# First MoE's combine inside the projection phase's tile loop, with a diagonal for 1/rms

## The chip, the cores and the metric

One NeuronCore of a Trainium2 chip runs the whole program once. The metric is device time in microseconds (us) of that execution, lower is better; a kernel is stated by the median of its runs. Engines are named as the profile names them: PE is TensorE, with its weight loads apart as PEld; DVE is VectorE, ACT is ScalarE, POOL is GpSimd, SP is SyncE, which here only starts DMA transfers.

## The reference

A two-layer decoder over T = 1040 tokens (16 meta tokens and 1024 of the input) of width 1024. Layer 0 is a state-space mixer and a mixture of experts (MoE). After it one K/V projection and layer 1's queries are taken from the residual stream `h`; layer 1 is a windowed attention and a second MoE. What matters here is how layer 0's MoE ends and what reads it:

```python
# hier_moe: every token goes to two of 32 experts
contrib = yb[dest] * sgate[:, None].astype(yb.dtype)
out = jnp.zeros_like(t).at[stok].add(contrib)

# reference
h = h + hier_moe(rmsnorm(h, norm_ffn[layer]), ...)          # layer 0
...
shared = shared_kv(rmsnorm(h, norm_kv), w_kv, b_kv)         # K and V, 256 columns each
q = (rmsnorm(h, norm_mix[1]) @ w_q + b_q)                   # 1024 columns

def rmsnorm(x, g):
    y = xf * lax.rsqrt(jnp.mean(xf * xf, axis=-1, keepdims=True) + RMS_EPS)
    return (y * g)
```

All three projections start from `h / rms(h)`; only the gains `norm_kv` and `norm_mix[1]` differ, and the kernel multiplies them into the weights.

## The kernel before

The program is a row of phases (`phase_mixer`, `phase_moe` for layer 0, `phase_project`, `phase_attend`, `phase_moe` for layer 1). Each phase is a block with one hand-written instruction stream for each engine; the streams meet only in semaphores, and at the end of a phase all engines meet, the phase's semaphores are cleared and the next block begins. So the order on each engine is that of the code. Tokens lie in 9 tiles: tiles 0 to 7 of 128 tokens, tile 8 (`XT`) of the 16 meta tokens. Float32 products are made of three passes over halves: a value is split into `hi` (ACT copies it to a rounded type) and `lo` (DVE subtracts), and PE adds hi·hi, lo·hi and hi·lo.

**End of `phase_moe`, layer 0.** Expert tiles are processed in a loop; each ends with a `down` product, an ACT copy to `y` (`store_y`, L1208) and a scatter by POOL to `y_dram` (L1129), of which one may be open at a time (`y_free`). When the last scatter has landed, SP loads for each token tile the pair of its expert outputs, 1 MB, into the place of the weight staging `raw` (L1040, six places, `NB`), and DVE adds them to `h` with the token's two gates (L1461, two instructions a tile). That is the combine. Then the phase ends.

**`phase_project`.** SP loads gains, three 512 KB column blocks of weights and biases. A loop over the 9 tiles follows: ACT squares the tile and sums (L1739), POOL makes `1/rms` in two small instructions (L1717, L1720), DVE multiplies `xn = h * rstd` (L1780), PE transposes it in eight pieces (L1827), ACT copies the result to `x_hi` (L1754), DVE subtracts to `x_lo` (L1771). POOL multiplies the gain into the first three weight blocks between the tiles (L1711). After the loop come the products, 12 column blocks of weights in order: K0, K1, then V (two blocks together, nine jobs of 128 or 16 tokens), then Q0 to Q7. The staging `raw` has three slots, `w_hi` and `w_lo` two each. A weight block passes through load (SP, after `w_lo_done` of the block three back), gain (POOL), `w_hi` (ACT, after PE has finished the block two back) and `w_lo` (DVE), and PE waits for that before its products (L1848). K and Q products have the weight as stationary operand and 512 tokens as moving one, V products have a token tile as stationary and 256 columns of weights as moving operand, 24 matmuls a job. DVE takes each result out of PSUM with its bias (L1805 for K, L1808 for V, L1810 for Q). In `phase_attend` PE runs for a while `spare_products(6)` (L2169), six plain float32 matmuls (ahead of the loop twelve, in one go) of 128 columns that nobody reads; the trace holds two rows for each of them.

Of the kernel before, what the change touches and what calls it, by code (L numbers as in the profile page):

```python
# [46 lines left out]

def tile_rows(i):

    return P if i < XT else N_META  # L50


def semaphore_source(nc, ctx, prefix):

    sems = []
# [10 lines left out]
    return sem  # L66

# [768 lines left out]
def phase_moe(nc, t, layer, out=None):  # L836
# [27 lines left out]
    with ExitStack() as ctx:  # L864
# [7 lines left out]

        ident = sb("ident", [P, P])
# [13 lines left out]
        gates = sb("gates", [P, 2, NT])  # L887
# [33 lines left out]
        raw = sb("raw", [P, 6, KC * F])  # L921
        hi, lo = (sb(x, [P, 3, KC * F], F32R) for x in ("hi", "lo"))
# [32 lines left out]
        yc_in = [sem(f"yc_in{b}") for b in range(NB)]  # L955
# [23 lines left out]
        def _(sp):  # L979
# [177 lines left out]
        def _(act):  # L1157
# [84 lines left out]
            store_y(n_q - 2, n_q * 6)  # L1242
            store_y(n_q - 1, n_q * 6 + 2)
# [8 lines left out]
        def _(dve):  # L1252
# [195 lines left out]
            hidden_lo_part(n_q - 1)  # L1448

# [7 lines left out]
            for i in range(NT):  # L1457
# [157 lines left out]
def phase_project(nc, t):  # L1615
# [7 lines left out]
    NP = 2 * KV // P + DC  # L1623
    K_P, V_P = KV // P, 2 * KV // P
    h, q_t, k_t, v_sb = t["h"], t["q_t"], t["k_t"], t["v_sb"]
    w_kv = t["w_kv"].rearrange("(p c) f -> p c f", c=DC)
    w_q = t["w_q"][0].rearrange("(p c) f -> p c f", c=DC)
    with ExitStack() as ctx:
        def sb(name, shape, dt=F32):
            return ctx.enter_context(nc.sbuf_tensor("prj_" + name, shape, dt))  # L1630

        sem = semaphore_source(nc, ctx, "prj_")
# [3 lines left out]
        sq = sb("sq", [P, D])  # L1636
        xn = sb("xn", [P, 2, D])
# [3 lines left out]
        g_kv, g_q = (sb(x, [P, DC]) for x in ("g_kv", "g_q"))  # L1641
        raw = sb("raw", [P, 3, DC, P])
        w_hi, w_lo = (sb(f"w_{x}", [P, 2, DC, P], F32R) for x in ("hi", "lo"))
        bk = sb("bk", [P, K_P])
# [5 lines left out]
        w_in = [sem(f"w_in{b}") for b in range(3)]  # L1650
        gains_in, bias_in, k_copied = (sem(x) for x in ("gains_in", "bias_in", "k_copied"))
        const_set, ident_step, squares_done, ss_scaled, rstd_done, xn_done, xt_mm, xt_hi, xt_lo = (
            sem(x) for x in ("const_set", "ident_step", "squares_done", "ss_scaled", "rstd_done", "xn_done",
# [19 lines left out]
        def _(sp):  # L1673
            def load(n):
                src = w_kv[:, :, n * P:(n + 1) * P] if n < V_P else w_q[:, :, (n - V_P) * P:(n - V_P + 1) * P]
                sp.dma_start(raw[:, n % 3], src).then_inc(w_in[n % 3], 16)

            for dst, src in ((g_kv, t["norm_kv"]), (g_q, t["norm_mix"][1])):
                sp.dma_start(dst[:, :], src.rearrange("(p c) -> p c", c=DC)).then_inc(gains_in, 16)
            for n in range(3):  # L1680
                load(n)
            sp.dma_start(bk[:, :], t["b_kv"][0:KV].rearrange("(c p) -> p c", p=P),
                         allow_slow_non_contiguous=True).then_inc(bias_in, 16)
            sp.dma_start(bq[:, :], t["b_q"][0].rearrange("(c p) -> p c", p=P),
                         allow_slow_non_contiguous=True).then_inc(bias_in, 16)
            sp.dma_start(bv[:, :], t["b_kv"][KV:].partition_broadcast(P)).then_inc(bias_in, 16)
            sp.wait_ge(squares_done, NT)
            sp.dma_start(sq[:, :], t["b_o"][0].partition_broadcast(P)).then_inc(bo_in, 16)
            for n in range(3, NP):
                sp.wait_ge(w_lo_done, n - 2)  # L1690
                load(n)
                if n == V_P:

                    sp.wait_ge(acc_free, jobs_before(K_P))
# [7 lines left out]
        def _(pool):  # L1702
# [3 lines left out]
            pool.wait_ge(gains_in, 32)  # L1706

            def gain(n):
                g = g_kv if n < V_P else g_q
                pool.wait_ge(w_in[n % 3], 16 * (n // 3 + 1))  # L1710
                nc.gpsimd.tensor_tensor(raw[:, n % 3], raw[:, n % 3],  # L1711
                                        g[:, :].unsqueeze(2).to_broadcast([P, DC, P]), ALU.mult).then_inc(gained, 1)

            for i in range(NT):
                n = tile_rows(i)
                pool.wait_ge(squares_done, i + 1)
                nc.gpsimd.tensor_scalar(ss[0:n, i:i + 1], ss[0:n, i:i + 1], 1.0 / D, EPS,  # L1717
                                        ALU.mult, ALU.add).then_inc(ss_scaled, 1)
                pool.wait_ge(ss_scaled, i + 1)
                nc.gpsimd.tensor_tensor(rstd[0:n, i:i + 1], ss[0:n, i:i + 1], mhalf[0:n, :],  # L1720
                                        ALU.pow).then_inc(rstd_done, 1)
                if i < 3:
                    gain(i)
            pool.wait_ge(bo_in, 16)
            pool.wait_ge(xn_done, NT)
            for n in range(3, NP):
                gain(n)
                if n >= V_P:
                    i = n - V_P
                    nc.gpsimd.tensor_tensor(h[:, i, :], h[:, i, :], sq[:, :], ALU.add).then_inc(bo_added, 1)  # L1730
# [3 lines left out]
        def _(act):  # L1734
            def squares(i):
                n = tile_rows(i)
                if i:
                    act.wait_ge(squares_done, i)
# [17 lines left out]
            for n in range(NP):  # L1756
                split_w(n)
# [468 lines left out]
```

## Time and profile before

| | us |
|---|---|
| median of the three runs (2241.44 to 2243.8) | 2242.67 |
| time of the execution that was profiled | 2243.16 |
| span of that execution in the trace | 2241.4 |
| PE busy in it | 1985.4 (89%) |
| DVE busy | 1586.7 (71%) |
| ACT busy | 1244.6 (56%) |
| POOL busy | 369.5 (16%) |
| last matmul of layer 0's MoE to first transpose of the projection: idle time of PE | 40.0 |
| first transpose to first product of the projection | 30.8 |
| first product to the end of the last | 152.3 |
| end of DVE's half of the last expert's fourth weight block (`lo_done` at `n_q * 6 - 2`), at | 1044.8 |

Times of instructions are microseconds from the start of the span. The profile is one execution. A timeline row gives start, length, engine, line, operation, tensors, shapes and the count of merged instructions; in square brackets stands how long the engine had been idle and who ended that. A matmul's length in a row holds its way through the array, so in a stream of matmuls the distance between starts tells more than the lengths. PEclk is the clock granted to PE, 1.00 for 2.4 GHz and 0.50 for 1.2 GHz.

### The profile page before, as it was taken

The page shows a single profiled execution, that of the slowest core. Times are in us where ns is not written, and L with a number is a line of the kernel's source. Part 1 is how long each engine was busy: PE and PEld are TensorE (multiplying, and loading weights), DVE is VectorE, ACT ScalarE, POOL GpSimd, SP SyncE. Part 2 cuts the span into 40 slices and gives each one's busy share as a digit, 9 for nine tenths or more (in the row PEclk, how much of TensorE's full clock was granted, in tenths as well). Part 3 has the DMA queues.
Part 4 walks back from the last instruction along what each step waited for, and adds up shares of the span by engine and source line. Part 5 has one row for each costly group of instructions (what it writes and reads, how often), then busy time and mean ns, then how long its engine had stood idle before and what let it go on. Part 6 is the DMA issues. An engine that isn't in the chain of part 4 may idle for free. (4 is left out here: it accounts for less than half of the span.)

```text
span 2241.4 us, 31742 instructions
## 1 busy us (share of the span) xinstructions
PE 1985.4 (89%) x10658; PEld 1572.3 (70%) x10658; DVE 1586.7 (71%) x1770; ACT 1244.6 (56%) x1521; POOL 369.5 (16%) x684
## 2 busy tenths in 40 slices
PE   4859999659999999999189999998599999999991
PEld 3558777548888888887178766666388888888880
DVE  8995221558888888887642276663688888888885
ACT  6524110437777777776120065554277777777772
POOL 2000000302211112221224000002022212112214
PEclk9979999879999999999579999999699999999995
DMA  3265100639999999996521020005299999999985
GB/s 98 36 60 176 63 1 1 248 113 365 381 375 371 367 373 374 377 376 253 189 67 38 10 86 1 1 1 198 103 343 360 360 375 385 378 384 387 383 315 235
DMA packets 136045, 504.69 MB, mean 225 GB/s; under 512 B 38466, under 2 KB 68498, under 8 KB 84754
## 3 DMA queue, kind: packets, MB, share of 16 engines
q1 hardware_dynamic: 116258, 468.85, 57.4%
q0 software_dynamic: 18432, 33.86, 4.0%
q10 hardware_dynamic: 1280, 0.98, 0.3%
q8 instruction: 47, 0.77, 0.1%
q14 instruction: 28, 0.23, 0.0%
HBM read 488.47 MB, written 47.32 MB: 239 GB/s over the span
## 5 line engine op out<-in xcount | busy, mean ns | idle before, releaser
L1406 DVE TENSOR_TENSOR moe_lo<-moe_raw,moe_hi 128x2048 fp32r<-128x2048 f32 x378 | 861.0, 2292 | 118.4 <-ACT moe_hi L1191 114.1
L1191 ACT CAST moe_hi<-moe_raw 128x2048 fp32r<-128x2048 f32 x374 | 714.2, 1915 | 153.5 <-PE moe_ps_g L1546 74.9
L1544 PE MATMUL moe_ps_g<-moe_hi,moe_x_hi 128*128 128x512 f32 x512 | 211.6, 413 | 7.2 <-DVE moe_x_lo L1411 4.7
L1544 PE MATMUL moe_ps_y<-moe_hi,moe_h_hi 128*128 128x512 f32 x512 | 209.0, 408 | 3.7 <-DVE moe_h_lo L1422 3.7
L1545 PE MATMUL moe_ps_g<-moe_hi,moe_x_lo 128*128 128x512 f32 x512 | 205.8, 402 | 0.0
L1546 PE MATMUL moe_ps_g<-moe_lo,moe_x_hi 128*128 128x512 f32 x512 | 205.3, 401 | 0.0
L1545 PE MATMUL moe_ps_y<-moe_hi,moe_h_lo 128*128 128x512 f32 x512 | 204.2, 399 | 0.0
L1546 PE MATMUL moe_ps_y<-moe_lo,moe_h_hi 128*128 128x512 f32 x512 | 203.9, 398 | 0.0
L1546 PE MATMUL moe_ps_u<-moe_lo,moe_x_hi 128*128 128x512 f32 x512 | 203.0, 396 | 0.0
L1544 PE MATMUL moe_ps_u<-moe_hi,moe_x_hi 128*128 128x512 f32 x512 | 202.8, 396 | 0.0
L1545 PE MATMUL moe_ps_u<-moe_hi,moe_x_lo 128*128 128x512 f32 x512 | 202.8, 396 | 0.0
L1198 ACT CAST moe_x_hi<-moe_ps_xt 128x1024 fp32r<-128x1024 f32 x64 | 65.1, 1017 | 157.2 <-PE moe_ps_xt L1531 157.2
L1544 PEld LDWEIGHTS moe_ps_g<-moe_hi,moe_x_hi 128*128 128x128 f32 x512 | 99.2, 194 | 29.9 <-DVE moe_x_lo L1411 5.5
L1411 DVE TENSOR_TENSOR moe_x_lo<-moe_ps_xt,moe_x_hi 128x1024 fp32r<-128x1024 f32 x64 | 78.4, 1225 | 52.3 <-ACT moe_x_hi L1198 52.3
L1544 PEld LDWEIGHTS moe_ps_y<-moe_hi,moe_h_hi 128*128 128x128 f32 x512 | 97.5, 191 | 25.2 <-DVE moe_lo L1406 4.0
L1546 PEld LDWEIGHTS moe_ps_g<-moe_lo,moe_x_hi 128*128 128x128 f32 x512 | 98.2, 192 | 24.0
L1546 PEld LDWEIGHTS moe_ps_y<-moe_lo,moe_h_hi 128*128 128x128 f32 x512 | 97.0, 189 | 23.6
L1545 PEld LDWEIGHTS moe_ps_u<-moe_hi,moe_x_lo 128*128 128x128 f32 x512 | 96.7, 189 | 23.6
L1545 PEld LDWEIGHTS moe_ps_g<-moe_hi,moe_x_lo 128*128 128x128 f32 x512 | 98.6, 192 | 20.9
L1544 PEld LDWEIGHTS moe_ps_u<-moe_hi,moe_x_hi 128*128 128x128 f32 x512 | 96.4, 188 | 23.5
L1546 PEld LDWEIGHTS moe_ps_u<-moe_lo,moe_x_hi 128*128 128x128 f32 x512 | 96.4, 188 | 23.2
L1545 PEld LDWEIGHTS moe_ps_y<-moe_hi,moe_h_lo 128*128 128x128 f32 x512 | 97.2, 190 | 20.7
(406 smaller groups left out, 3699.1 us busy)
## 6 DMA issues: line engine op xcount, KB each, us to landing
moe_raw<-moe_w_gate SPq DMA_DIRECT2D x128, 1024.0 KB, 7.3
moe_raw<-moe_w_up SPq DMA_DIRECT2D x128, 1024.0 KB, 8.0
moe_raw<-moe_w_down SPq DMA_DIRECT2D x128, 1024.0 KB, 7.3
moe_raw<-y_dram SPq DMA_DIRECT2D x16, 1024.0 KB, 11.6
mix_r<-ssm_w_glu SPq DMA_DIRECT2D x16, 512.0 KB, 5.2
xn_dram<-moe_work SPq DMA_DIRECT2D x16, 512.0 KB, 7.4
mix_r<-x SPq DMA_DIRECT2D x8, 512.0 KB, 5.4
mix_r<-h_dram SPq DMA_DIRECT2D x16, 256.0 KB, 11.6
```

Source lines behind the costliest of these rows:

```text
L1191: A.copy(hi[:, slot(number, k), :], raw[:, k, :]).then_inc(hi_done, 1)
L1198: A.copy(x_hi[:, :, :].rearrange("p c m -> p (c m)"), ps_xt[:, :]).then_inc(xt_hi, 1)
L1406: V.tensor_tensor(lo[:, slot, :], raw[:, k, :], hi[:, slot, :].bitcast(F32), ALU.subtract).then_inc(lo_done, 1)
L1411: V.tensor_tensor(x_lo[:, :, :].rearrange("p c m -> p (c m)"), ps_xt[:, :], x_hi[:, :, :].bitcast(F32).rearrange("p c m -> p (c m)"), ALU. ...
L1544: T.matmul(out, x_h, w_h, start=first, stop=False)
L1545: T.matmul(out, x_l, w_h, start=False, stop=False)
L1546: return T.matmul(out, x_h, w_l, start=False, stop=final)
```

## The change

It does four things.

1. The combine leaves `phase_moe` of layer 0. SP still issues the first four pair loads there, into `yc`, a ring of four places (`N_YC`) over memory that held `hi` and `lo`; the other five are issued in `phase_project`, each after the tile four back is combined. The semaphores `yc_in` and the tensors `gates`, `yc` outlive the phase. Tiles now come in the order 8, 0, 1 to 7 (`TILE_ORDER`).
2. In the tile loop DVE combines a tile, and the product `xn = h * rstd` is gone. DVE instead writes `scale`, the identity times `rstd` (128x128), and PE multiplies `h` by it, which transposes and scales at once: eight plain float32 matmuls in the place of eight transposes.
3. The V products of a tile (24 matmuls) follow in the same loop, one tile behind; DVE takes them out of PSUM in the loop too. V comes before K.
4. The four weight blocks of K and V are loaded, multiplied by their gain (now by DVE) and split at the end of `phase_moe`, after the last expert's halves. Weights have a ring of four slots (`W_KV`), with `w_lo` written in place over `w_raw`. A Q block's load waits until PE has finished the block four back.

The biases and the query gain are loaded by ACT's queue; `b_o` and the squares use the memory of `gain`.

```diff
@@ phase_moe
+                sp.dma_start(g_kv[:, :], t["norm_kv"].rearrange("(p c) -> p c", c=DC)).then_inc(wkv_in, 16)
+                sp.wait_ge(lo_done, n_q * 6 + (-2))
+                for n in range(W_KV):
+                    sp.dma_start(t["w_raw"][:, n], kv_columns(t, n)).then_inc(wkv_in, 16)
             sp.wait_ge(y_free, n_q + 1)
-            for i in range(NT):
+            if not last_layer:
+                for j in range(N_YC):
+                    load_pair(sp, t, j)
+            for i in range(NT if last_layer else 0):
...
             store_y(n_q - 2, n_q * 6)
+            if not last_layer:
+                for n in range(W_KV):
+                    act.wait_ge(gained, n + 1)
+                    A.copy(t["w_hi"][:, n], t["w_raw"][:, n]).then_inc(wkv_hi, 1)
             store_y(n_q - 1, n_q * 6 + 2)
...
             hidden_lo_part(n_q - 1)
+            if not last_layer:
+                dve.wait_ge(wkv_in, 16 * (W_KV + 1))
+                for n in range(W_KV):
+                    V.tensor_tensor(t["w_raw"][:, n], t["w_raw"][:, n], g_kv[:, :].unsqueeze(2).to_broadcast([P, DC, P]),
+                                    ALU.mult).then_inc(gained, 1)
+                for n in range(W_KV):
+                    dve.wait_ge(wkv_hi, n + 1)
+                    V.tensor_tensor(t["w_lo"][:, n], t["w_raw"][:, n], t["w_hi"][:, n].bitcast(F32),
+                                    ALU.subtract).then_inc(wkv_lo, 1)
@@ phase_project, SP
+            for j in range(N_YC, NT):
+                sp.wait_ge(h_new, 2 * (j - N_YC + 1))
+                load_pair(sp, t, j)
             sp.wait_ge(squares_done, NT)
             sp.dma_start(sq[:, :], t["b_o"][0].partition_broadcast(P)).then_inc(bo_in, 16)
-            for n in range(3, NP):
-                sp.wait_ge(w_lo_done, n - 2)
-                load(n)
+            for n in range(Q0, NC):
+                sp.wait_ge(acc_done, jobs_to(n - W_KV))
+                sp.dma_start(w_raw[:, n % W_KV], w_q[:, :, (n - Q0) * P:(n - Q0 + 1) * P]).then_inc(w_in[n % W_KV], 16)
@@ phase_project, ACT
+            for j in range(NT):
+                squares(j)
+                if j >= 1:
+                    hi_part(j - 1)
+            hi_part(NT - 1)
@@ phase_project, DVE
-                V.tensor_scalar(xn[0:n, i % 2, :], h[0:n, i, :], rstd[0:n, i:i + 1], None,
-                                ALU.mult).then_inc(xn_done, 1)
+            def set_scale(j):
+                i = TILE_ORDER[j]
+                n = tile_rows(i)
+                dve.wait_ge(rstd_done, j + 1)
+                if j >= 2:
+                    dve.wait_ge(xt_mm, j - 1)
+                V.tensor_scalar(scale[0:n, j % 2, 0:n], ident[0:n, 0:n], rstd[0:n, i:i + 1], None,
+                                ALU.mult).then_inc(scale_set, 1)
...
+            for j in range(NT + 3):
+                if j < NT:
+                    combine(j)
+                if 1 <= j <= NT:
+                    set_scale(j - 1)
+                if 2 <= j <= NT + 1:
+                    lo_part(j - 2)
+                if j == 3:
+                    dve.wait_ge(bias_in, 48)
+                if j >= 3:
+                    values(j - 3)
@@ phase_project, PE
-                for c in range(DC):
-                    last = T.transpose(ps_x[:, i % 2, c * P:c * P + n],
-                                       xn[0:n, i % 2, :].rearrange("p (m c) -> p c m", c=DC)[:, c, :],
-                                       ident[0:n, 0:n])
+                for c in range(DC):
+                    last = T.matmul(ps_x[:, j % 2, c * P:c * P + n],
+                                    h[0:n, i, :].rearrange("p (m c) -> p c m", c=DC)[:, c, :],
+                                    scale[0:n, j % 2, 0:n], start=True, stop=True)
...
+            for j in range(NT):
+                turn(j)
+                if j >= 1:
+                    value_product(j - 1)
+            value_product(NT - 1)
```

DVE's instructions from the last expert's half into the projection phase. Before (`moe_h_lo` is that half, L1461 the combine, L1780 the scaled tile):

```order
L1422 TENSOR_TENSOR moe_h_lo<-moe_ps_ht,moe_h_hi 128x512
L1461 SCALAR_TENSOR_TENSOR h<-moe_raw,moe_gates,h 128x1024 x16
L1461 SCALAR_TENSOR_TENSOR h<-moe_raw,moe_gates,h 16x1024 x2
L864 UNCONDITIONAL_BRANCH
L1759 UNCONDITIONAL_BRANCH
L1780 TENSOR_SCALAR prj_xn<-h,prj_rstd 128x1024 x2
L1771 TENSOR_TENSOR prj_x_lo<-prj_ps_x,prj_x_hi 128x8x128
```

And in the changed kernel, up to the first full round of the loop:

```order
L1460 TENSOR_TENSOR moe_h_lo<-moe_ps_ht,moe_h_hi 128x512
L1490 TENSOR_TENSOR w_raw<-w_raw,moe_g_kv 128x1024 x4
L1494 TENSOR_TENSOR w_lo<-w_raw,w_hi 128x1024 x4
L886 UNCONDITIONAL_BRANCH
L1797 UNCONDITIONAL_BRANCH
L1806 SCALAR_TENSOR_TENSOR h<-yc,gates,h 16x1024 x2
L1806 SCALAR_TENSOR_TENSOR h<-yc,gates,h 128x1024 x2
L1816 TENSOR_SCALAR prj_scale<-prj_ident,prj_rstd 16x16
L1806 SCALAR_TENSOR_TENSOR h<-yc,gates,h 128x1024 x2
L1816 TENSOR_SCALAR prj_scale<-prj_ident,prj_rstd 128x128
L1823 TENSOR_TENSOR prj_x_lo<-prj_ps_x,prj_x_hi 128x8x16
L1806 SCALAR_TENSOR_TENSOR h<-yc,gates,h 128x1024 x2
```

The combine crossed the phase's end and now alternates with the scale and the halves; the eight weight instructions stand in its old place.

SP's queue at the same place. Before:

```order
L1030 DMA moe_raw<-moe_w_down 128x2048
L1036 REGISTER_ALU
L1040 DMA moe_raw<-y_dram 128x2048 x8
L1040 DMA moe_raw<-y_dram 16x2048
L864 UNCONDITIONAL_BRANCH
L1672 UNCONDITIONAL_BRANCH
L1679 DMA prj_g_kv<-norm_kv 128x8
L1679 DMA prj_g_q<-norm_mix 128x8
L1676 DMA prj_raw<-w_kv 128x8x128 x3
```

And in the changed kernel:

```order
L1055 DMA moe_raw<-moe_w_down 128x2048
L1062 DMA moe_g_kv<-norm_kv 128x8
L1063 REGISTER_ALU
L1065 DMA w_raw<-w_kv 128x8x128 x4
L1067 REGISTER_ALU
L86 DMA yc<-y_dram 16x2048
L86 DMA yc<-y_dram 128x2048 x3
L886 UNCONDITIONAL_BRANCH
L1719 UNCONDITIONAL_BRANCH
L86 DMA yc<-y_dram 128x2048 x5
L1725 DMA gain<-b_o 128x1024
L1728 DMA w_raw<-w_q 128x8x128 x4
```

The weight loads stand ahead of the pair loads, and five of the nine pair loads stand behind the phase's end.

## Rows read from the trace of the kernel before

**Rows 1.** Stretches: us, busy PE, PEld, DVE, ACT, POOL, PEclk, DMA share, GB/s.
```profile
1070.00:1103.00 33.00, 0.00 (x0) 0.00 (x0) 23.10 (x18) 2.30 (x4) 0.95 (x5) 0.50 0.64 260
1103.00:1135.00 32.00, 16.79 (x72) 13.51 (x72) 20.88 (x20) 17.59 (x25) 12.21 (x20) 0.50 0.25 68
```

**Rows 2.** Timelines of SP, DVE and POOL over the phase's end; start us, length us.
```profile
1069.75 3.06 SPq L1040 DMA_DIRECT2D moe_raw<-y_dram  x6
...
1074.44 18.45 DVE L1461 SCALAR_TENSOR_TENSOR h<-moe_raw,moe_gates,h 128x1024 f32<-128x1024 f32 x14 [17.76 <-DMA moe_raw<-y_dram]
1093.74 5.22 DVE L1461 SCALAR_TENSOR_TENSOR h<-moe_raw,moe_gates,h 128x1024 f32<-128x1024 f32 x4 [0.84 <-DMA moe_raw<-y_dram]
...
1100.30 0.10 POOL L1703 MEMSET prj_mhalf<- 128x1 f32 x1 [30.57 <-POOLq L59]
```

**Rows 3.** Timeline of PE: first products of K0, of V, of Q0.
```profile
1135.10 0.77 PE L1848 MATMUL prj_acc<-prj_x_hi,prj_w_hi 128*128 128x512 f32 x1 [2.65 <-DVE prj_w_lo L1765]
...
1167.27 0.55 PE L1848 MATMUL prj_acc<-prj_w_hi,prj_x_hi 128*128 128x256 f32 x1 [2.50 <-DVE prj_w_lo L1765]
...
1198.15 0.50 PE L1848 MATMUL prj_acc<-prj_x_hi,prj_w_hi 128*128 128x512 f32 x1 [2.45 <-DVE prj_w_lo L1765]
```

**Rows 4.** Timeline: ACT's square, DVE's half, PE's eight transposes; POOL's `b_o` after it.
```profile
1122.70 1.06 ACT L1739 ACTIVATE prj_sq<-h 128x1024 f32<-128x1024 f32 x1
...
1125.56 1.23 DVE L1771 TENSOR_TENSOR prj_x_lo<-prj_ps_x,prj_x_hi 128x1024 fp32r<-128x1024 f32 x1
...
1125.60 1.97 PE L1827 MATMUL prj_ps_x<-prj_ident,prj_xn 128*128 128x128 f32 x8 [1.12 <-DVE prj_xn L1780]
...
1144.18 2.41 POOL L1730 TENSOR_TENSOR h<-h,prj_sq 128x1024 f32<-128x1024 f32 x1
```

**Rows 5.** Timeline of PE: twelve plain float32 matmuls in 24 rows, and eight transposes.
```profile
1289.75 2.94 PE L2169 MATMUL att_ps_y<-att_ident 128*128 128x128 f32 x24
...
1612.79 1.05 PE L1531 MATMUL moe_ps_xt<-moe_ident,moe_xg 128*128 128x128 f32 x8
```

**Rows 6.** Timeline of DVE: K's and V's results taken out of PSUM.
```profile
1162.22 1.78 DVE L1805 TENSOR_SCALAR k_t<-prj_acc,prj_bk 64x384 f32<-64x384 f32 x4 [3.78 <-PE prj_acc L1848]
1164.80 1.08 DVE L1805 TENSOR_SCALAR k_t<-prj_acc,prj_bk 64x16 f32<-64x16 f32 x6 [0.80 <-PE prj_acc L1848]
...
1175.97 0.43 DVE L1808 TENSOR_TENSOR v_sb<-prj_acc,prj_bv 128x256 f32<-128x256 f32 x1 [2.78 <-PE prj_acc L1848]
1178.81 0.42 DVE L1808 TENSOR_TENSOR v_sb<-prj_acc,prj_bv 128x256 f32<-128x256 f32 x1 [2.42 <-PE prj_acc L1848]
```

**Rows 7.** Stretches, PE alone (busy, PEclk, DMA share, GB/s): V's start, all of Q.
```profile
1167.20:1173.40 6.20, 6.13 (x29) 0.50 1.00 239
...
1198.10:1287.40 89.30, 89.24 (x384) 1.00 0.10 30
```

**Rows 8.** Timelines of DVE and POOL in the second MoE's combine, at its end.
```profile
2213.78 2.60 DVE L1461 SCALAR_TENSOR_TENSOR h<-moe_raw,moe_gates,h 128x1024 f32<-128x1024 f32 x2
...
2215.20 1.59 POOL L1154 TENSOR_TENSOR moe_rstd<-moe_ss,moe_mhalf 128x1 f32<-128x1 f32 x1
...
2234.38 0.55 POOL L1154 TENSOR_TENSOR moe_rstd<-moe_ss,moe_mhalf 128x1 f32<-128x1 f32 x1
```

**Rows 9.** End of the first MoE: DVE, ACT, POOL, and the K/V weight loads' landing.
```profile
1055.99 0.68 DVE L1422 TENSOR_TENSOR moe_h_lo<-moe_ps_ht,moe_h_hi 128x512 fp32r<-128x512 f32 x1
...
1064.36 1.01 ACT L1211 COPY moe_y<-moe_ps_y 128x1024 f32<-128x1024 f32 x1 [7.74 <-PE moe_ps_y L1546]
...
1065.53 0.18 POOL L1113 COPY moe_si<-moe_idx_out 128x1 int32 x1 [4.48 <-ACT moe_y L1211]
...
prj_raw<-w_kv SPq DMA_DIRECT2D x4, 512.0 KB, 5.7
```

**Rows 10.** Stretches of the second MoE's routing, all engines, columns as in Rows 1.
```profile
1555.00:1565.00 10.00, 7.88 (x64) 6.85 (x63) 6.44 (x8) 8.10 (x9) 2.60 (x4) 1.00 1.02 427
1565.00:1575.00 10.00, 7.02 (x43) 5.70 (x43) 7.57 (x15) 3.04 (x3) 0.00 (x0) 0.83 1.01 402
```

More of the change, by code:

```diff
@@ L1455, in final_scale @@
                                        ALU.mult).then_inc(fin_done, 1)
-            for i in range(NT):
+            for i in range(NT if last_layer else 0):
                 n = rows(i)
@@ L1640, in phase_project @@
         x_hi, x_lo = (sb(f"x_{x}", [P, DC, TOK], F32R) for x in ("hi", "lo"))
[L1641 to L1644, printed above, removed]
+        g_q = sb("g_q", [P, DC])
+        bk = sb("bk", [P, K0])
         bq = sb("bq", [P, DC])
@@ new lines, in hi_part @@
+            def hi_part(j):
+                i = TILE_ORDER[j]
+                n = tile_rows(i)
+                act.wait_ge(xt_mm, j + 1)
+                A.copy(x_hi[:, :, i * P:i * P + n],
+                       ps_x[:, j % 2, :].rearrange("p (c m) -> p c m", c=DC)[:, :, 0:n]).then_inc(xt_hi, 1)
+            for j in range(NT):
[3 more added lines that the diff above has]
+            hi_part(NT - 1)
+            for n in range(Q0, NC):
+                act.wait_ge(gained, n - Q0 + 1)
+                A.copy(w_hi[:, n % W_KV], w_raw[:, n % W_KV]).then_inc(w_hi_done, 1)
@@ L1787, in _ @@
-            k = 0
-            for n in range(NP):
-                ahead = n + 1 < NP and n != V_P - 1
-                if ahead:
+            dve.wait_ge(ident_step, 2)
+            for j in range(NT + 3):
[9 more added lines that the diff above has]
+                    values(j - 3)
@@ L1791, in _ @@
+            k = NT
+            for n in range(K0, NC):
+                if Q0 <= n + 1 < NC:
                     split_w(n + 1)
@@ new lines, in value_product @@
+            def value_product(j):
+                pe.wait_ge(xt_lo, j + 1)
+                i = TILE_ORDER[j]
+                product(j, 0, i * P, tile_rows(i))
+            for j in range(NT):
[3 more added lines that the diff above has]
+            value_product(NT - 1)
+            k = NT
+            for n in range(K0, NC):
+                if n >= Q0:
+                    pe.wait_ge(w_lo_done, n - Q0 + 1)
+                for at, m in jobs(n):
+                    product(k, n, at, m)
@@ L2206, in program @@
         phase_mixer(nc, t)
+        t["gates"] = ctx.enter_context(nc.sbuf_tensor("gates", [P, 2, XT + 1], F32))
+        t["yc"] = nc.alloc_sbuf_tensor_at("yc", [P, N_YC, 2, D], F32, offset=-(-nc.sbuf_base // 32) * 32)
+        for name, at, dt in (("w_raw", RAW_AT + 2 * 8192, F32), ("w_lo", RAW_AT + 2 * 8192, F32R),
+                             ("w_hi", RAW_AT + 4 * 8192, F32R)):
+            t[name] = nc.alloc_sbuf_tensor_at(name, [P, W_KV, DC, P], dt, offset=at)
+        t["yc_in"] = [nc.alloc_semaphore(name=f"yc_in{b}") for b in range(N_YC)]
         phase_moe(nc, t, 0)
```

232 lines of the change are left out of this document (112 added, 120 removed).

## The prediction, made before the result was known

> **What bounds the kernel now.** Read the stretches first. Between 1070 and 1103 us PE does nothing, and between 1103 and 1135 it is busy 16.8 of 32 us with transposes at a clock of 0.50 [rows 1]. So the edge between the first MoE and the products costs some 65 us, in which PE has little to do, and every microsecond of it is on the path, since nothing of the later phases can start.
>
> The timelines say what ends last in it. The scatter is through at 1069.7, the first pair of expert outputs lands 4.7 us after its issue, DVE combines from 1074.44 to 1098.96, and 1.34 us later the next phase begins [rows 2]. Then the tile loop runs, and PE starts on products at 1135.10. Two more waits lie in the weight pipeline, 2.50 us before V and 2.45 before Q [rows 3]; after the first of them the clock is 0.50 again for 6.2 us [rows 7]. From 1198.1 to 1287.4 the Q products run without a gap at 1.00 [rows 7]; there nothing can be gained.
>
> **What the change takes away.** I don't add up savings but build the new time line from 1069.7 to the end of the Q products, 1287.4 before, and take the difference.
>
> *End of the MoE.* The V weights now have to be split before this edge. The K/V loads took 5.7 us at the median [rows 9]; four are issued from 1044.8 on (the table's last line), 11 us before DVE's last half at 1055.99 [rows 9], and should have landed. DVE's four gains and four halves are the size of L1771's, 1.23 us [rows 4], 9.8 us together, and run from 1056.7 to 1066.5, in time in which DVE was idle. What hides them is the last `down` product and the scatter; ACT's four copies (1.01 us each, as its copy of `y` of the same size, so through at about 1062.7) stand ahead of that last copy of `y` at 1064.36 [rows 9], with 1.6 us to spare. One thing is not hidden. In the second MoE's combine a POOL instruction of 0.55 us takes 1.59 while DVE works on two tensors in SBUF [rows 8]; it ends only when DVE's instruction has ended. POOL's step before the last scatter, 1065.53 [rows 9], now meets DVE's last half, which ends at 1066.5. I charge 0.9 us (bounds 0 and 3, if POOL's instructions of the scatter before meet DVE as well and the y buffer comes free late).
>
> *Start of the loop.* First load issued at 1070.65; four issues at 0.51 us (six in 3.06 [rows 2]) to 1072.7; 1.34 for the phase's end, 1074.0. The first data can be there at 1070.65 + 4.7 = 1075.3, which is later. A tile's combine is 2 x 1.32 = 2.64 us (14 in 18.45 [rows 2]). Tiles 8 and 0 are combined by 1080.6. The 1/rms of the first one is held up by DVE as above, so that the scale comes 0.8 later, 1081.4 (the scale itself is not in the trace; `xn` with eight times the columns bounds it at 0.75 us, I take 0.2). Third combine 1084.0, scale 0.6 later: PE can turn the first full tile at 1084.6.
>
> *The loop.* DVE has per tile 2.64 + 0.2 + 1.23 + 0.42 = 4.5 us [rows 2, 4, 6]. PE has the turn and the V job. The V job is 2.84 us, from one result to the next [rows 6]. The turn is eight plain float32 matmuls of 128 columns with 128-column weights. The nearest row is of just that form: twelve of them take 2.94 us, so eight take 1.96; eight transposes take 1.05 [rows 5], the lower bound. Sum 4.8 us, so PE is the bound, by a little. It should run almost without gaps from 1084.6, because `turn` of the next tile fills the time in which ACT and DVE make the halves of this one, and its own need is met in time: counted from the end of turn j-2, DVE gets the V result at 2.84 and has the scale of tile j ready 0.42 + 2.64 + 0.2 later, at 6.1, while PE wants it at 2.84 + 1.96 + 2.84 = 7.6. So 8 turns 15.7 us, 9 V jobs 25.6 us (the one for 16 tokens streams the same columns), waits of 0.1 a tile 0.8 us. It starts at half clock. Before V the clock rose after 6.2 us of work [rows 7], before K after 4; that loses 3.1 or 2.0 us, I take 2.6. The last V job ends at 1084.6 + 15.7 + 25.6 + 0.8 + 2.6 = 1129.3.
>
> *K and Q.* A job of 24 matmuls with 512 columns takes 89.3 / 16 = 5.57 us [rows 7], one with 16 columns 2.58 [rows 6]. K is 4 x 5.57 + 2 x 2.58 = 27.5, Q 89.1. With four slots Q0's load starts at the end of V and has the 27.5 us of K to pass through load (5.7), gain and `b_o` on POOL (2.4 each at most [rows 4]), copy and half (2.2); later blocks have more than 11 us of slack. So no waits: 1129.3 + 27.5 + 89.1 = 1245.9.
>
> 1287.4 - 1245.9 = 41.5 us less. The profiled execution would go from 2243.2 to 2201.7, and since the median of the runs lies 0.5 below it, I predict 2201 us.
>
> **POOL and DVE.** [Rows 8] speak against the change: in the old loop DVE's `xn` reads one SBUF tensor, in the new one the combine reads two, and it is on while POOL makes 1/rms. The Trainium skill states it too (GPSIMD Engine Reference, Specifications): GpSimd's way to SBUF is shared with VectorE, with contention when a DVE instruction has two SBUF inputs. The trace agrees, 1.59 us for 0.55. In steady state it costs nothing by my order: after combine j DVE has 1.9 us of scale, half and V result, while the square takes 1.06 [rows 4] and its sum a little more, and POOL 0.8, and the scale is needed only after combine j+1.
>
> **The price of a plain float32 matmul.** The transposes that go are cheap and what replaces them is not: 1.96 against 1.05 us [rows 5]. The Trainium skill (TensorE: Matmul & The Clock Gate, Terms) says that the transpose mode is four times as fast for FP32. By that the turn would cost 4.2 us instead of 1.96, 17.9 more over eight tiles, 2219 us. The row of the same form says no; I keep it as a rival.
>
> **The rivals.**
>
> A, the forecast: the loop runs at PE's pace of 4.8 us. 2201, own range 2195 to 2208. 70%.
>
> B, the loop goes at the pace of a chain instead: scale held up by POOL (up to 1.0), the half waiting for ACT, which stands behind a square. Then a tile takes 5.4 to 6.5 us; seven intervals more at 0.6 to 1.7 are 4 to 12 us, 2205 to 2213. For it: the two engines are so close (4.5 and 4.8) that any delay shows. Against: the 1.5 us of slack just counted. 13%.
>
> C, PE's clock stays at 0.50 through the loop. V jobs 24 x 6.13 / 29 = 5.1 us [rows 7], turns 1.97 [rows 4] x 1.96 / 1.05 = 3.7. Then 8 x 3.7 + 9 x 5.1 = 75.5 after 1084.6, end at 1160.1 + 2.5 to warm up + 116.6 = 1279.2, 8 less than before: 2234. For it: with PE 70% busy the clock was 0.83 [rows 10], so it falls where gaps come. Against: at half clock PE is behind and has no gaps at all, which is how it rose before K and V, and at 79% busy it was granted 1.00 [rows 10]. 5%.
>
> D, slower than before: half clock, and PE waits each tile for copy and half of the same tile (1.01 + 1.23). Then a tile takes 3.7 + 5.1 + 2.2 = 11.0 us. It decides at 10.0 us a tile: 1084.6 + 7 x 10.0 + 13.9 + 119.1 = 1287.6, the old end. At 11.0 the time is 2250. Against it stands that `turn` of the next tile is ahead of the V job in PE's order. 3%.
>
> E, better than forecast: turns near 1.05 us. Then DVE's 4.5 is the pace, the end of V is 1084.6 + 7 x 4.5 + 1.1 + 5.7 = 1122.9, 6.4 earlier, 2195; with no loss at the scatter 2194. 7%.
>
> F, the turn at 4.2 us as above, 2219. 2%.
>
> That the change doesn't do what it says has a small form only: if the K/V blocks landed after 1060, ACT's last copy of `y` would wait for `w_hi` and all would move by that. It is in A's range.
>
> **How the numbers follow.** Range 2193 to 2213: it holds nearly all of A, B and E and leaves out C, D, F and the tails, somewhat under 20%. Faster by more than 0.2% (4.5 us, about what a measurement can tell from no change): A, B, C, E and F, 96 to 97%; slower D, 3%; in between about 1%, between C and D.
>
> **What would show it.** Right: turns of about 2 us and V jobs every 4.8 to 4.9 us on PE between 1085 and 1130, clock 1.00 after the first tiles; last V result near 1129; no wait for `w_lo` after it; Q's end near 1246. DVE should wait for ACT's copy, not PE for the scale. Wrong: POOL's two instructions at 1.3 to 1.6 us in steady state with PE waiting behind the scale (B); PEclk of 0.5 between 1090 and 1125 (C, D); turns of 1 or of 4 us (E, F); ACT's last copy of `y` later than 1064.4.

## The result, and the profile after

| | before | after |
|---|---|---|
| median of the runs shown, us | 2243.24 (4 runs, 2241.44 to 2245.32) | 2214.11 (4 runs, 2212.98 to 2215.36) |
| span of the profiled execution | 2241.4 | 2212.9 |
| start of the projection phase on POOL | 1100.30 | 1076.39 |
| last V result taken out of PSUM, start | 1195.74 | 1143.44 |
| last Q result taken out of PSUM, start | 1287.43 | 1260.73 |

The ratio is 0.987, with a 95% interval of 0.9856 to 0.9884: 29.1 us less, where 41.5 were forecast. The forecast time was 2201, with a range to 2213; the median lies 1.1 above that. Three of the stations in the table carry the reading: V's end was forecast at 1129.3 and came at 1143.4; from there to Q's end took 117.3 us, where 116.6 were forecast. So nearly the whole miss lies ahead of V's end (14.1 us there, 0.7 behind it).

PE's timeline of the changed kernel, the rows of the turn (those of V between them are left out):

```profile
1083.16 8.00 PE L1886 MATMUL prj_ps_x<-prj_scale,h 16*128 16x16 f32 x32 [20.13 <-DVE prj_scale L1816]
...
1093.81 3.98 PE L1886 MATMUL prj_ps_x<-prj_scale,h 128*128 128x128 f32 x16
...
1100.45 3.98 PE L1886 MATMUL prj_ps_x<-prj_scale,h 128*128 128x128 f32 x16
...
1107.11 3.98 PE L1886 MATMUL prj_ps_x<-prj_scale,h 128*128 128x128 f32 x16
```

One turn is 16 rows, two for each of eight matmuls, and it stands every 6.66 us. V's share of that is 2.82, so a turn is 3.84, not 1.96. The row that I had taken the price from [rows 5] is one of *the same shape and type*. The difference shows in the weight loads, in the groups of the two lines (shortest, median and longest length in ns, first and last start); the second group holds the spare products of [rows 5] in the changed kernel:

```profile
L1886 PEld LDWEIGHTS prj_ps_x<-prj_scale,h x144: 307/336/338, 1083.2 to 1137.2; 128*128 128x128 f32 x128, 16*128 16x128 f32 x16
```

```profile
L2242 PEld LDWEIGHTS att_ps_y<-att_ident x120: 186/192/192, 1263.1 to 1290.4; 128*128 128x128 f32 x120
```

DVE's timeline of one round answers to [rows 4, 6]:

```profile
1107.65 2.60 DVE L1806 SCALAR_TENSOR_TENSOR h<-yc,gates,h 128x1024 f32<-128x1024 f32 x2
1110.29 0.29 DVE L1816 TENSOR_SCALAR prj_scale<-prj_ident,prj_rstd 128x128 f32<-128x128 f32 x1
1112.17 1.23 DVE L1823 TENSOR_TENSOR prj_x_lo<-prj_ps_x,prj_x_hi 128x1024 fp32r<-128x1024 f32 x1 [1.60 <-ACT prj_x_hi L1785]
1113.97 0.42 DVE L1831 TENSOR_TENSOR v_sb<-prj_acc,prj_bv 128x256 f32<-128x256 f32 x1 [0.57 <-PE prj_acc L1904]
```

It works 4.5 us a round and waits for 2.2, first for ACT's copy of the turn, then for V: both times PE is behind it. The stretches say the same (busy us of PE, PEld, DVE, ACT, POOL, then PEclk, DMA share, GB/s): PE has no gap.

```profile
1084.00:1100.00 16.00, 16.00 (x91) 15.42 (x91) 10.46 (x13) 5.44 (x9) 4.77 (x7) 0.80 0.65 235
1100.00:1110.00 10.00, 10.00 (x59) 10.00 (x57) 7.16 (x9) 2.06 (x3) 1.45 (x4) 1.00 0.11 48
1110.00:1120.00 10.00, 10.00 (x66) 10.00 (x66) 6.12 (x8) 4.12 (x6) 0.81 (x3) 1.00 0.00 0
```

The phase's edge, which answers to [rows 2, 9], is the second place. POOL's timeline:

```profile
1057.02 1.09 POOL L1147 COPY moe_si<-moe_idx_out 128x1 int32 x1 [9.04 <-ACT moe_y L1245]
1058.18 1.06 POOL L1150 TENSOR_TENSOR moe_unit<-moe_mhalf 128x1 f32<-128x1 f32 x1
1059.39 1.81 POOL L1163 DMA_INDIRECT y_dram<-moe_y,moe_si  x1
...
1066.47 1.00 POOL L1163 DMA_INDIRECT y_dram<-moe_y,moe_si  x1
1069.80 0.18 POOL L1167 TENSOR_TENSOR moe_unit<-moe_mhalf 128x1 f32<-128x1 f32 x1 [2.33 <-DMA y_dram<-moe_y,moe_si]
1076.39 0.10 POOL L1740 MEMSET prj_mhalf<- 128x1 f32 x1 [6.40 <-POOLq L65]
```

And the instruction that fills that idle time, in the group of the phase's block (it stands once at the end of each MoE):

```profile
L886 POOLq DRAIN  x2: 5560/5740/5919, 1069.8 to 2205.8; - x2
```

SP had issued its four pair loads by 1071.8; then every engine waits for POOL's DRAIN until 1075.4. The kernel before has it too, from 1069.5 to 1075.1: there it lay under the wait for the first pair (until 1074.44) and the first instruction of the combine [rows 2].

### The profile page after: what moved, and what is told of

Read it like the earlier page. It is cut to its first block and busy times, and to the rows that moved or that the text cites. A ratio compares the mean times of both kernels' runs of the same rounds, so it can differ in the third digit from the quotient of the medians.

```text
span 2212.9 us, 31883 instructions
## 1 busy us (share of the span) xinstructions
PE 1993.8 (90%) x10730; PEld 1586.2 (72%) x10730; DVE 1582.4 (72%) x1774; ACT 1243.6 (56%) x1521; POOL 368.4 (17%) x680
```

## The experiments

Unless said otherwise each differs from the changed kernel by its edit alone, and its output is the reference's. "Round" is the distance between two combines in DVE's timeline. The profiled executions differ ahead of this place too: the projection phase starts on POOL at 1073.18 in `e4_v_after` and at 1076.39 in the changed kernel, with the same code up to there. So stations of two kernels are compared from the phase's start on, not from the span's.

### The turn's price: where the columns lie

The turn reads `h` as its stationary operand with every eighth column (`"p (m c) -> p c m"`); the spare products of [rows 5] read neighbouring ones. The first experiment gives the channels another order, so that the eight pieces are neighbouring columns, and loads `w_kv`, `w_q` and the two gains in that order. Theory S is the stride.

```diff
-    return t["w_kv"].rearrange("(p c) f -> p c f", c=DC)[:, :, at:at + P]
+    return t["w_kv"].rearrange("(c p) f -> p c f", c=DC)[:, :, at:at + P]
...
-                                    h[0:n, i, :].rearrange("p (m c) -> p c m", c=DC)[:, c, :],
+                                    h[0:n, i, c * P:(c + 1) * P],
```

> The changed kernel with one thing different: the projection's channels are taken as (c p) in the place of (p c), for weights, gains and the turn, so that the turn's stationary operand is 128 neighbouring columns of h and not every eighth one. What is computed is the same. Theory S (the stride of the stationary operand is what makes the turn take 3.84 us instead of 1.96): the turn's weight loads take 0.19 us instead of 0.34, the turn 1.9 us, a tile 4.8 us instead of 6.66, and the median falls by 8 x 1.86 = 15 us, from 2214 to 2199. Rival P (a plain float32 matmul on h costs 0.48 us however the operand lies, the cheap row was a special case): no change, 2214.

2199.45 us, ratio 0.9798 (0.9782 to 0.9815). PE's timeline:

```profile
1095.86 1.95 PE L1888 MATMUL prj_ps_x<-prj_scale,h 128*128 128x128 f32 x16
...
1100.47 1.95 PE L1888 MATMUL prj_ps_x<-prj_scale,h 128*128 128x128 f32 x16
...
1105.07 1.95 PE L1888 MATMUL prj_ps_x<-prj_scale,h 128*128 128x128 f32 x16
```

The same 16 rows take 1.95 us where they took 3.98, both by the row's length, and the forecast from [rows 5] was 1.96. A round is 4.61, so that by distance, without V's 2.82, a turn is 1.79. Now DVE waits 0.21 us a round in all, so the two engines stand as close together as the prediction had them.

The second measures the form by itself. Behind the twelve spare products ahead of the attention's loop it adds eight groups of twelve more, on `q_t`, that nobody reads: neighbouring columns of `q_t`, then every 2nd, 4th and 8th, transposes of neighbouring ones and of every 8th, and `q_t` as moving operand with neighbouring columns and with every 8th. The first group is:

```diff
+            for _ in range(12):
+                T.matmul(ps_y[:, 0:P], qf[:, 0:P], ident[:], start=True, stop=True)
...
```

> The changed kernel with eight groups of twelve unused matmuls of 128 columns put behind the twelve spare ones ahead of the attention, one form to a line: plain float32 with 128 columns of q as stationary operand, neighbouring, then every second, every fourth, every eighth; two groups of transposes, neighbouring and every eighth; two plain ones with the identity as stationary and q as moving operand, neighbouring and every eighth. The output is not touched. Theory S (stride of the stationary operand of a plain float32 matmul): group 1 at 0.24 us a matmul, group 4 at 0.48, transposes 0.12 in both, moving stride no effect or a smaller one; groups 2 and 3 tell whether the price grows with the stride or comes at once. Rival P (data other than the identity): group 1 already at 0.48.

One run, 2241.63 us beside 2243.91 before it. PE's timeline:

```profile
1262.70 2.94 PE L2242 MATMUL att_ps_y<-att_ident 128*128 128x128 f32 x24
1265.48 2.84 PE L2251 MATMUL att_ps_y<-att_ident,q_t 128*128 128x128 f32 x24
1268.16 2.99 PE L2253 MATMUL att_ps_y<-att_ident,q_t 128*128 128x128 f32 x24
1270.99 5.76 PE L2255 MATMUL att_ps_y<-att_ident,q_t 128*128 128x128 f32 x24
1276.59 5.87 PE L2257 MATMUL att_ps_y<-att_ident,q_t 128*128 128x128 f32 x24
1282.30 1.47 PE L2259 MATMUL att_ps_y<-att_ident,q_t 128*128 128x128 f32 x12
1283.61 1.50 PE L2261 MATMUL att_ps_y<-att_ident,q_t 128*128 128x128 f32 x12
1284.94 2.84 PE L2263 MATMUL att_ps_y<-q_t,att_ident 128*128 128x128 f32 x24
1287.62 5.76 PE L2265 MATMUL att_ps_y<-q_t,att_ident 128*128 128x128 f32 x24
```

Read the distances between starts; the clock was 1.00 throughout. Neighbouring columns (L2242, L2251) and every second (L2253) cost 2.7 to 2.8 us for twelve matmuls; every fourth and eighth (L2255, L2257) 5.6 to 5.7. As moving operand (L2263, L2265) it is the same, 2.7 and 5.7, where I had expected no effect or a smaller one. Transposes (L2259, L2261) cost 1.3 either way. A step of 4 or 8 columns doubles a plain float32 matmul, a step of 2 doesn't (3 wasn't tried), and a step of 8 leaves a transpose alone. Why the step costs this wasn't tried. That settles theory S; its rival fell with the first of the two experiments.

### The second part undone: DVE makes `xn`, PE transposes

```diff
-                V.tensor_scalar(scale[0:n, j % 2, 0:n], ident[0:n, 0:n], rstd[0:n, i:i + 1], None,
+                V.tensor_scalar(xn[0:n, j % 2, :], h[0:n, i, :], rstd[0:n, i:i + 1], None,
...
-                    last = T.matmul(ps_x[:, j % 2, c * P:c * P + n],
-                                    h[0:n, i, :].rearrange("p (m c) -> p c m", c=DC)[:, c, :],
-                                    scale[0:n, j % 2, 0:n], start=True, stop=True)
+                    last = T.transpose(ps_x[:, j % 2, c * P:c * P + n],
+                                       xn[0:n, j % 2, :].rearrange("p (m c) -> p c m", c=DC)[:, c, :],
+                                       ident[0:n, 0:n])
```

> The changed kernel with its second part alone undone: DVE writes xn = h * rstd (0.75 us) and PE transposes it, in the combined loop. Theory: PE's tile is then 1.05 + 2.84 = 3.9 us and DVE is the bound with 2.64 + 0.75 + 1.23 + 0.42 = 5.04 and small gaps, 5.2 us a tile instead of 6.66, median 2214 - 8 x 1.45 = 2202 to 2203. Rival 1, PE's clock falls because PE now idles a quarter of the time: PEclk under 0.9 between 1095 and 1130, tile of 6 to 8 us, 2210 or more. Rival 2, POOL's instructions are held up by DVE's two-input combine and PE waits for xn: tile of 5.7, 2206.

2198.2 us, ratio 0.9796 (0.978 to 0.9812), 4 us below the expectation. DVE's timeline:

```profile
1096.88 2.60 DVE L1806 SCALAR_TENSOR_TENSOR h<-yc,gates,h 128x1024 f32<-128x1024 f32 x2
1099.52 0.75 DVE L1816 TENSOR_SCALAR prj_xn<-h,prj_rstd 128x1024 f32<-128x1024 f32 x1
1100.18 1.22 DVE L1823 TENSOR_TENSOR prj_x_lo<-prj_ps_x,prj_x_hi 128x1024 fp32r<-128x1024 f32 x1
1101.32 0.42 DVE L1831 TENSOR_TENSOR v_sb<-prj_acc,prj_bv 128x256 f32<-128x256 f32 x1
1101.65 2.60 DVE L1806 SCALAR_TENSOR_TENSOR h<-yc,gates,h 128x1024 f32<-128x1024 f32 x2
```

DVE is now the bound and runs without a gap, 4.77 us a round where 5.2 were expected. PEclk is 1.00 from 1095 to 1130, so the first rival fell too. So the diagonal, as the change writes it, costs 15.9 us against its own undoing: it takes 0.46 us a tile from DVE, which has time, and puts 2.8 on PE, which has none.

### The third part undone: V after the loop

```diff
-            for j in range(NT + 3):
+            for j in range(NT + 2):
...
-                if j >= 3:
-                    values(j - 3)
+            for j in range(NT):
+                values(j)
...
-                if j >= 1:
-                    value_product(j - 1)
-            value_product(NT - 1)
+            for j in range(NT):
+                value_product(j)
```

> The changed kernel with its third part alone undone: the V products follow after the tile loop. Theory (PE bounds the loop with 6.66 = 3.84 + 2.82): without V the loop goes at DVE's 4.3 us, and V adds 9 x 2.84 = 25.6 us behind it, so V ends near 1086.5 + 7 x 4.3 + 3.8 + 2.4 + 25.6 = 1148.4, 5 us later than in the changed kernel, median 2219. Rival (V in the loop is hidden behind DVE, as it would be with a turn of 2 us): taking it out costs most of its 25 us, 2235 or more. If the clock falls in the loop it adds 2 to 8 us to either.

2219.45 us, ratio 0.9891 (0.9875 to 0.9908), 5.3 us above the changed kernel. With PE as the bound, V's place matters only through PE's gaps: in a stretch of the loop PE is busy 8.77 of 10 us, at a clock of 0.83. PE does two turns every 9.3 us, 4.65 a turn, where the expectation had 4.3. From the phase's start to the last V result it is 72.1 us, against 67.0 in the changed kernel.

```profile
1100.00:1110.00 10.00, 8.77 (x37) 8.52 (x36) 8.50 (x9) 4.12 (x6) 3.88 (x5) 0.83 0.00 0
```

### `xn` on ACT: an order that loses, and one that wins

ACT is the idlest of the three. In these two it makes `xn` (activation with a scale), and PE transposes. They have the same instructions; ACT's order in a round differs. The first:

```diff
+                A.activation(xn[0:n, j % 2, :], h[0:n, i, :], ACT.Copy, scale=rstd[0:n, i:i + 1]).then_inc(scale_set, 1)
...
+            for j in range(NT + 2):
+                if j < NT:
+                    squares(j)
+                if 1 <= j <= NT:
+                    scaled(j - 1)
+                if j >= 2:
+                    hi_part(j - 2)
```

> As the run before it, but ACT makes xn (about 1.06 us) and DVE neither xn nor the scale. Busy time per tile: DVE 2.64 + 1.23 + 0.42 = 4.3, ACT 1.25 + 1.06 + 1.01 = 3.3, PE 3.9. Theory: the loop goes at DVE's pace, about 4.5 us a tile, median 2214 - 8 x 2.15 = 2197. Rival, the chain square, 1/rms, xn, turn, copy, half is too long for the two buffers: a tile of 5.5 us, 2205.

A miss: 2213.9 us, ratio 0.9867 (0.985 to 0.9883), no better than the changed kernel. ACT's and then DVE's timeline:

```profile
1102.91 1.06 ACT L1779 ACTIVATE gain<-h 128x1024 f32<-128x1024 f32 x1 [4.20 <-DVE h L1816]
1103.87 0.19 ACT L1779 ACTIVATION_READ_ACCUMULATOR gain<-h 128x1 f32 x1
1103.96 1.13 ACT L1794 ACTIVATE prj_xn<-h,prj_rstd 128x1024 f32<-128x1024 f32 x1
1105.00 0.99 ACT L1785 CAST prj_x_hi<-prj_ps_x 128x1024 fp32r<-128x1024 f32 x1
```

```profile
1100.28 2.59 DVE L1816 SCALAR_TENSOR_TENSOR h<-yc,gates,h 128x1024 f32<-128x1024 f32 x2
1106.10 1.23 DVE L1833 TENSOR_TENSOR prj_x_lo<-prj_ps_x,prj_x_hi 128x1024 fp32r<-128x1024 f32 x1 [3.22 <-ACT prj_x_hi L1785]
```

ACT waits for DVE's combine, DVE waits for ACT's copy, each in every round: the copy that DVE wants stands behind a square that wants DVE's combine of the same round. The round is the sum of this circle, combine 2.6, then 3.2 on ACT, then half and V result, 7.29 us. The copy itself could have been made long before. I had counted each engine's work and not followed the queue. The test of this is to change the order alone (the diff is against `e3_xn_act`):

```diff
-            for j in range(NT + 2):
...
+            for j in range(NT):
+                squares(j)
+                if j >= 1:
+                    hi_part(j - 1)
+                scaled(j)
+            hi_part(NT - 1)
```

> The same instructions as e3_xn_act (ScalarE makes the normalized tile, TensorE transposes it); only ScalarE's order in a round differs: squares of tile j, upper part of tile j-1, normalized tile j, where e3 had squares j, normalized j-1, upper part j-2. Theory O (e3 lost its gain to its queue order: VectorE waited 3.22 us in each round for an upper part that stood behind two ScalarE instructions which themselves waited for VectorE's combine): now the upper part that VectorE wants was copied one round earlier, so VectorE runs back to back, 2.60 + 1.23 + 0.42 = 4.25 to 4.5 us a round where e3 had 7.29, and the time is e2_xn_dve's 2198 less some 0.3 us in each of 9 rounds: 2194 to 2197. Rival (ScalarE is too slow for the work, whatever the order, or VectorE and ScalarE disturb each other on the same tile): a round stays over 6 us and the time at 2208 to 2214.

2194.78 us, ratio 0.9781 (0.9766 to 0.9796). DVE's timeline:

```profile
1096.67 2.60 DVE L1815 SCALAR_TENSOR_TENSOR h<-yc,gates,h 128x1024 f32<-128x1024 f32 x2
1099.31 1.22 DVE L1832 TENSOR_TENSOR prj_x_lo<-prj_ps_x,prj_x_hi 128x1024 fp32r<-128x1024 f32 x1
1100.45 0.41 DVE L1840 TENSOR_TENSOR v_sb<-prj_acc,prj_bv 128x256 f32<-128x256 f32 x1
1100.78 2.60 DVE L1815 SCALAR_TENSOR_TENSOR h<-yc,gates,h 128x1024 f32<-128x1024 f32 x2
```

4.11 us a round for 7.29 of the same work. The circle was the cause.

### POOL's DRAIN at the phase's edge

If all engines stand until 1075.4, work can be put there. The combine of the 16-token tile (2.6 us) goes to the end of `phase_moe`:

```diff
@@ phase_moe, DVE, behind w_lo
+                dve.wait_ge(t["yc_in"][0], 16)
+                for k in range(2):
+                    V.scalar_tensor_tensor(h[0:N_META, XT, :], t["yc"][0:N_META, 0, k, :], gates[0:N_META, k, XT:XT + 1],
+                                           h[0:N_META, XT, :], ALU.mult, ALU.add).then_inc(h_new, 1)
+                    dve.wait_ge(h_new, k + 1)
@@ phase_project
-                if j < NT:
+                if 1 <= j < NT:
                     combine(j)
```

> The changed kernel, with the combine of the first, 16-row tile (two VectorE instructions, 2.60 us together) done by VectorE at the end of the MoE phase, behind the last splits of w_kv, in place of the start of the projection phase. Theory D (between the last scatter and the first instruction of the projection phase all engines wait for GpSimd's DRAIN of 5.56 us, from 1069.8 to 1075.4, and nothing else is left to do there): the two combines lie wholly under the drain, the first turn starts 2.6 us sooner, and the loop, at 6.66 us a round with TensorE always busy, ends 2.6 us sooner: 2211.5. Rival (the end of the drain moves with the last VectorE work, or what comes after it is set by the identity matrix and the DMAs of the new phase): no gain, 2214, or a loss of up to 2.6 us if VectorE's work holds GpSimd's drain up.

> e2_xn_dve (VectorE makes the normalized tile, TensorE transposes it) and e7_head_in_moe together. Under theory D the gains add, since VectorE sets e2's pace of 4.77 us a round from its first combine on: 2198.2 - 2.6 = 2195.6. Rival: 2198.

2216.33 us (ratio 0.9879, 0.9864 to 0.9894) and 2198.02 us (0.98, 0.9786 to 0.9813): nothing gained, either on the changed kernel or on `e2_xn_dve`. The combine did run under the DRAIN but for its end: it starts when its load lands, at 1072.15, and ends at 1074.73, some 0.2 us behind the DRAIN, and the phase starts 7.0 us after POOL's last instruction in place of 6.4. Then ACT's timeline of the first of the two shows what was late next:

```profile
1076.06 0.41 ACTq L1772 DMA_DIRECT2D prj_bv<-b_kv  x1
1076.50 0.46 ACTq L1773 DMA_DIRECT2D prj_bk<-b_kv  x1
1076.98 0.49 ACTq L1775 DMA_DIRECT2D prj_bq<-b_q  x1
1077.50 2.76 ACTq L1777 DMA_DIRECT2D prj_g_q<-norm_mix  x1
1080.31 1.05 ACT L1785 ACTIVATE gain<-h 16x1024 f32<-16x1024 f32 x1 [16.29 <-issue]
```

ACT issues four loads ahead of its first square, until 1080.3. In the changed kernel that ended at 1078.9, and the square waited for the combine until 1079.7 anyway. The next two kernels give all four to SP as well (the diff shows `bv`):

```diff
@@ phase_project, ACT
-            A.dma_start(bv[:, :], t["b_kv"][KV:].partition_broadcast(P)).then_inc(bias_in, 16)
...
@@ phase_project, SP, behind the fifth pair load
+                if j == N_YC:
+                    sp.dma_start(bv[:, :], t["b_kv"][KV:].partition_broadcast(P)).then_inc(bias_in, 16)
...
```

> e7_head_in_moe, and with it the four loads of biases and gains that ScalarE issues at the start of the projection phase (in e7 from 1076.06 to 1080.26, 4.1 us, 2.76 of them the last one) are issued by SyncE's queue instead, behind its load for the fifth tile. Theory Q (e7 gained nothing because ScalarE, with h of the first tile ready since 1074.7, issued its loads until 1080.3 and only then squared, so the two microseconds won ahead of the phase were spent there): the first square starts at the phase's start, 1076.1, the first turn at about 1079.8 where e7 had 1082.87 and the changed kernel 1083.16, and the time is 2214.1 - 3 = 2211. Rival (the loop's pace absorbs an earlier start, since TensorE begins at the lower clock anyway or GpSimd and VectorE set the first rounds): 2214 to 2216.

> e6_act_order with both moves of e9_head_and_issues. VectorE sets e6's pace of 4.1 us a round and waits only in the first rounds. Theory Q: the first combine of a 128-row tile starts at the phase's start in place of 2.6 us behind it, and ScalarE is ready for its square: 2194.8 - 2.7 = 2192. Rival: 2195.

2211.86 us (ratio 0.9859, 0.9844 to 0.9874) and 2191.06 us (0.9763, 0.975 to 0.9776), both as theory Q has it. In the first of them ACT's square comes with the phase's start on POOL, 1074.21, and the first turn 4.2 us after that, where `e7_head_in_moe` had 6.8:

```profile
1074.23 1.06 ACT L1786 ACTIVATE gain<-h 16x1024 f32<-16x1024 f32 x1 [11.70 <-PEq L65]
```

The gain is small beside the intervals, so the traces must carry it: from the phase's start on POOL to the last V result it is 67.0 us in the changed kernel, 68.1 with the combine moved, 65.0 with the loads moved too; and 48.0 in `e6_act_order`, 45.1 in `e10_all`. The last is the fastest kernel of this study, 23 us below the changed one.

## Why the prediction was off

Its own steps, against the trace of the changed kernel.

**The turn, 1.96 us: the step that failed.** It measured 3.84. Eight turns are 30.7 us where 15.7 were forecast, 15.0 more. I took "of just that form" for proof because shapes and types agreed; the rows' text doesn't hold the stride, the code does, and the code was before me. The two experiments on columns show the cause and its size: undone, the time is 2199.5, in the forecast's own range. By the distance of starts its turn is 1.79 and its V job 2.82, where 1.96 and 2.84 were forecast.

**The rival F** had nearly this time, 2219, at 2%, from the rule that the Trainium skill gives (TensorE: Matmul & The Clock Gate, Terms), that the transpose mode is four times as fast for FP32; its turn of 4.2 us stands 0.4 above the measured 3.84. The runs show both: a transpose is 1.3 us for twelve; a plain matmul costs four times that with every fourth or eighth column and twice that with neighbouring ones. The rule holds here for the strided operand only, and that was this operand.

**The start, 1084.6.** The first full turn starts when the first, small one ends, near 1087.0: 2.4 late. Two errors. The phase's end was put at 1.34 us after SP's last issue, read from a place where the first load and DVE's combine hid POOL's DRAIN; uncovered it sets the phase's start, 1076.4 for 1074.0, and the first combine, 1077.1 for 1075.3. That is 1.8 us, net of a last scatter that ended 0.6 us earlier than forecast (below). 0.7 of it is the combine's wait for POOL's identity matrix, which only the scale reads; moving that wait wasn't tried. The other 0.6 is the small turn, which has as many rows as a full one and takes 3.9 us at this stride; I had not put it in PE's way. The full one's scale was ready at 1086.4.

**Cold clock and waits, 3.4 us.** They took 0.3: 8 x 3.84 + 9 x 2.82 = 56.1 of the 56.4 us from 1087.0 to 1143.4. The clock was 0.50 until 1090.4, as expected, but a strided turn doesn't run slower for that (last section). So this term was spared by the same stride that broke the first: in `e1_contiguous` the first two turns took 7.0 us at 0.50, against 3.6 for two later ones.

**The scatter, +0.9.** DVE did hold POOL: 1.81 us for the indirect DMA that takes 1.00 undisturbed, 1.06 for 0.19. It fell mostly on the scatter before the last one. ACT's last copy of `y` had to wait for that and stood at 1063.87, 0.8 behind the end of PE's last `down` product, and POOL's copy for the last scatter took 1.01 us for 0.18. That is 1.6 us, not 0.9 (bound 3). Still the copy of `y` was ahead of the old 1064.36 [rows 9], and the last scatter ended at 1069.98, only +0.3, because that `down` product ended 1.3 us sooner than in the kernel before, 1063.04 for 1064.33. There the clock had fallen, here it didn't. What decides between the two isn't shown, and nothing in the forecast counted on it. The stretches, all engines, before and then after:

```profile
1057.00:1060.00 3.00, 3.00 (x8) 2.36 (x9) 0.00 (x0) 0.00 (x0) 1.20 (x2) 0.56 0.21 82
1057.00:1060.00 3.00, 2.83 (x12) 2.34 (x13) 3.00 (x3) 1.83 (x2) 2.75 (x3) 1.00 0.00 0
```

**The loop's logic held.** PE is the bound; DVE waits for ACT's copy (1.60 us) and for V's result, as forecast; POOL's two instructions are at 0.19 and 0.55 us in steady state; only in the first three rounds the second takes 1.45 to 1.62 and the first up to 0.75, where DVE waits 0.5 us for each. The scale took 0.29, not 0.2, off the path.

**K and Q, 116.6.** 117.3, and no wait for `w_lo`: four slots do take the waits of [rows 3] away.

The sum: Q's end was forecast 41.5 us earlier and came 26.7 earlier. The 14.8 are +15.0 for the turns, +2.4 for the start, -3.1 for cold clock and waits, -0.2 for V, +0.7 for K and Q. The start and the cold clock nearly cancel, and that is luck. What follows Q took 954.0 us before and 952.2 after, which gives 1.8 back. The kernels here lie between 952 and 954 in that stretch, and I can't tie this to the change.

Of the change's four parts, the third is worth 5.3 us. The second costs 15.9 as written (2214.1 against 2198.2); with neighbouring columns it would be 2199.5 against 2198.2, which can't be told apart. The 5.3 are the third part's worth only where the strided turn fills PE. In `e2_xn_dve` V's jobs lie in time that PE has free. An estimate from its rows: with V behind the loop the last transpose would end near 1114, nine jobs of 2.83 us follow, and the last V result would come near 1139 in place of 1125.5, so about 14 us. The combine's move and the weights' early load were not undone alone. `e2_xn_dve` has them and the third part and is 45.0 us below the kernel before, so by that estimate some 30 us are theirs together. How they share them stays open, and no run shows the estimate.

## What to carry to other kernels

A row prices another instruction only if the operands' strides agree too, and these stand in the code, not in the row. When a stretch of work is moved off a phase's edge, list everything that ran in its shadow, queue drains and DMA issues included, for one of them is late next. And count a loop not by each engine's work alone: follow which instruction stands behind which in each queue; two engines that each waited for the other's instruction of the same round cost the sum of both, 7.29 us for 4.11.

## What the runs showed of the hardware

- A plain float32 matmul of 128 columns with a 128-column stationary operand cost 0.22 to 0.24 us with columns 1 or 2 elements apart, and 0.47 to 0.48 with every 4th or 8th, at a clock of 1.00; the 8th was tried on either operand. A transpose cost 0.11 with neighbouring columns and with every 8th (`e5_forms`, one run).
- The strided price was the same at both levels of PE's clock. The 32 rows of the first two turns take 7.8 us, 0.24 each, at a clock of 0.50, and the 16 rows of a later turn 3.84, also 0.24 each, at 1.00. With neighbouring columns the two are apart: in `e1_contiguous` the first 32 rows took 7.0 us, 0.22 each, at 0.50, and a later turn 1.79, 0.11 each, at 1.00, all by the distance of starts. The first 16 of the 32 rows are in both kernels those of the 16-token tile. The stretches of the changed kernel for this line (busy PE, PEclk, DMA share, GB/s; the count is of rows in the stretch):

```profile
1088.00:1089.00 1.00, 1.00 (x6) 0.50 1.01 426
...
1094.80:1095.80 1.00, 1.00 (x6) 1.00 0.00 0
```

- POOL's DRAIN at the end of a MoE phase takes 5.56 (first) and 5.92 us (second), with and without work of DVE beside it (before, changed kernel, `e7_head_in_moe`, `e9_head_and_issues`, `e10_all`), and at the first one no engine gets into the next phase before it ends. At the ends of the changed kernel's other phases it takes 3.39 (mixer), 0.05 (projection) and 0.28 (attention). Only the MoE phases use indirect DMAs, but what makes it long wasn't tried.
- ACT's issue of the 1024 gains took 1.05 us in the changed kernel, 0.60 in `e2_xn_dve` and `e6_act_order`, and 2.76 and 2.40 in `e7_head_in_moe` and `e8_dve_and_head`, where SP's fifth pair load is issued at the phase's start. That this load is the cause wasn't tried.
